# Weight units of the second block rounded and completed by GpSimd's own memory transfers

## The reference, cut to what matters

```python
h = rms_norm_2(x, norm_g)
proj = h @ w_in                                    # (512, 1024) @ (1024, 9 k)
(a_u, a_v, a_z, b_q, b_c, b_qi, b_ki, b_wi, b_z,
 c_b, c_c, c_x, c_z, d_q, d_k, d_v, d_f, d_z, gates) = jnp.split(proj, points, axis=-1)
y_a = chunked_spatial_gating(a_u, a_v, ...) * jax.nn.silu(a_z)
y_b = dsa_attention(b_q, b_c, b_qi, b_ki, b_wi, ...) * jax.nn.silu(b_z)   # top-k of scores, sparse attention
y_c = short_gated_conv(c_b, c_c, c_x, conv_w) * jax.nn.silu(c_z)
y_d = forgetting_attention(d_q, d_k, d_v, d_f, fox_b_f) * jax.nn.silu(d_z)
branch_d = jnp.einsum('nbsw,nwd->bsnd', ys, w_branch)
merged = jnp.sum(jax.nn.sigmoid(gates) * branch_d, axis=2)
return x + merged @ w_out
```

## Time and profile before

| | |
|---|---|
| time, median of 3 runs | 1111.63 us (1111.48 to 1111.64) |
| span of the profiled execution, first to last instruction | 1109.4 us |
| busy: TensorE / VectorE / ScalarE / GpSimd | 1100.7 / 744.2 / 506.9 / 19.8 us |
| weight loads of TensorE | 931.1 us |
| read from memory, written | 115.74 MB, 4.19 MB |
| mean rate, share of the 16 engines used by SyncE's queue | 109 GB/s, 29.7% |

### The profile page before, as it was taken

How to read it: one execution, slowest core, us unless ns; L and a number is a source line. 1 busy time by engine, 2 the same in 40 slices (tenths; PEclk the granted TensorE clock), 3 DMA queues, 4 the chain that set the end, 5 groups by cost and what they waited for, 6 DMA issues and landing times.

```text
span 1109.4 us, 18066 instructions
## 1 busy us (share of the span) xinstructions
PE 1100.7 (99%) x7344; PEld 931.1 (84%) x7344; DVE 744.2 (67%) x1195; ACT 506.9 (46%) x851; POOL 19.8 (2%) x40
## 2 busy tenths in 40 slices
PE   9999999999999999999999999999999999999997
PEld 8888888888888888878888887887789999999986
DVE  6875876864686247448789896447568677667853
ACT  7562354324675225533342434336544444444543
POOL 1000000000001001000000000000000000000000
PEclk9999999999999999999999999999999999999999
DMA  9543324432215433522223232231121322333241
GB/s 372 220 149 125 125 68 133 127 102 73 74 58 167 139 95 111 185 74 79 77 76 95 77 95 68 66 114 58 58 73 61 114 93 80 115 115 114 81 186 76
DMA packets 33618, 121.09 MB, mean 109 GB/s; under 512 B 3824, under 2 KB 3824, under 8 KB 33536
## 3 DMA queue, kind: packets, MB, share of 16 engines
q1 hardware_dynamic: 30672, 109.88, 29.7%
q0 software_dynamic: 2720, 10.03, 2.7%
q10 hardware_dynamic: 144, 0.03, 0.0%
HBM read 115.74 MB, written 4.19 MB: 108 GB/s over the span
## 4 chain that ended last, share of the span: by engine, by line
PE 98%; DMA 1%; DVE 1%; ACT 0%; SPq 0%; issue 0%; ACTq 0%
PE acc L1829 22%; PE acc L1831 21%; PE acc L1830 21%; PE acc L1841 2%; PE side L1841 2%; PE acc L1839 2%; PE side L1839 2%; PE acc L1837 2%; PE side L1837 2%; PE acc L2189 2%; PE side L1829 2%; PE side L1830 2%; PE side L1831 2%; PE side L2071 2%; PE side L1984 2%; PE side L2189 1%
## 5 line engine op out<-in xcount | busy, mean ns | idle before, releaser
L1160 DVE TENSOR_TENSOR w_lo<-raw,w_hi 128x1024 fp32r<-128x1024 f32 (+2 forms) x194 | 225.8, 1165 | 149.7 <-ACT w_hi L649 146.8
L1829 PE MATMUL acc<-hT_hi,w_hi 128*128 128x512 f32 x648 | 258.9, 400 | 0.0
L1831 PE MATMUL acc<-hT_hi,w_lo 128*128 128x512 f32 x648 | 252.8, 390 | 0.0
L1830 PE MATMUL acc<-hT_lo,w_hi 128*128 128x512 f32 x648 | 252.4, 390 | 0.0
L649 ACT ACTIVATE w_hi<-raw 128x1024 fp32r<-128x1024 f32 (+2 forms) x194 | 195.6, 1009 | 115.4 <-PE acc L1831 87.7
L1829 PEld LDWEIGHTS acc<-hT_hi,w_hi 128*128 128x128 f32 x648 | 121.9, 188 | 26.9 <-issue 2.9
L1831 PEld LDWEIGHTS acc<-hT_hi,w_lo 128*128 128x128 f32 x648 | 121.6, 188 | 26.1
L1830 PEld LDWEIGHTS acc<-hT_lo,w_hi 128*128 128x128 f32 x648 | 121.9, 188 | 23.6
L1829 PE MATMUL acc<-w_hi,hT_hi 128*128 128x512 f32 (+1 forms) x152 | 60.3, 396 | 0.0
L1831 PE MATMUL acc<-w_hi,hT_lo 128*128 128x512 f32 (+1 forms) x152 | 58.8, 387 | 0.0
L1830 PE MATMUL acc<-w_lo,hT_hi 128*128 128x512 f32 (+1 forms) x152 | 58.7, 386 | 0.0
(11 more groups left out here) (461 smaller groups left out, 2251.5 us busy)
## 6 DMA issues: line engine op xcount, KB each, us to landing
raw<-in_ga SPq DMA_DIRECT2D x32, 512.0 KB, 4.5
ada_raw<-in_ada SPq DMA_DIRECT2D x16, 512.0 KB, 11.5
raw<-in_wo SPq DMA_DIRECT2D x16, 512.0 KB, 3.5
raw<-in_br SPq DMA_DIRECT2D x16, 512.0 KB, 3.5
raw<-in_q SPq DMA_DIRECT2D x8, 512.0 KB, 3.5
raw<-in_u SPq DMA_DIRECT2D x8, 512.0 KB, 4.0
raw<-in_gp SPq DMA_DIRECT2D x8, 512.0 KB, 4.5
raw<-in_ada_w SPq DMA_DIRECT2D x8, 512.0 KB, 3.6
```

What stands on the lines that cost most here:

```text
L1160: nc.vector.tensor_tensor(out=lo[:, 0:width], in0=strip_of(k), in1=hi[:, 0:width].bitcast(f32), op=ALU.subtract).then_inc(lo_made, 1)
L1829: nc.tensor.matmul(ps, w[0], x[0], start=first, stop=False)
L1830: nc.tensor.matmul(ps, w[0], x[1], start=False, stop=False)
L1831: return nc.tensor.matmul(ps, w[1], x[0], start=False, stop=last)
```

## The change

The 44 units leave `ORDER`, so SyncE no longer loads them and they no longer pass through `raw`. GpSimd gets a loop over them (`FED`). For a unit k it waits until `unit_used` is k - 3 and issues a transfer from memory straight into `w_hi`, whose type makes the transfer round. ScalarE, where it rounded before, waits for that transfer and writes -w_hi into `w_lo`. GpSimd waits for that (`negated`), and for the last adding transfer before it (`fed_lo`), and issues a second transfer of the same unit into `w_lo` that adds: w_lo = w - w_hi. TensorE waits for this one. VectorE's subtraction is gone for these units. `parts_made(k)` counts the units up to k that are still made in the old way; waits on `hi_made` and `lo_made` use it.

```diff
+FED_KINDS = ("au", "az", "cc", "cx", "cb", "cz", "dq", "dk", "dv", "bz", "dz")
+UNITS = [u for u in ORDER if u[0] not in ADA]
+ORDER = [u for u in ORDER if u[0] not in FED_KINDS]
...
+FED = [k for k, u in enumerate(USED) if u[0] in FED_KINDS]
+def parts_made(k):
+    return sum(1 for n in range(k + 1) if n not in FED)
+def fed_before(k):
+    return FED.index(k) + 1
...
@@ SyncE
-                        sp.wait_ge(lo_made, raw_done(last) + 1)
+                        sp.wait_ge(lo_made, parts_made(raw_done(last)))
...
@@ GpSimd, behind the loop that cuts the score tiles
+            for k in FED:
+                kind, j = USED[k]
+                pool.wait_ge(unit_used, k - SPLITS + 1)
+                pool.dma_start(w_hi[:, k % SPLITS, :], dram[kind][j, :, :]).then_inc(fed_hi, 16)
+                pool.wait_ge(negated, fed_before(k))
+                if fed_before(k) > 1:
+                    pool.wait_ge(fed_lo, 16 * (fed_before(k) - 1))
+                pool.dma_start(w_lo[:, k % SPLITS, :], dram[kind][j, :, :], accum_op=ALU.add).then_inc(fed_lo, 16)
...
@@ ScalarE, split_hi
+                if k in FED:
+                    act.wait_ge(fed_hi, 16 * fed_before(k))
+                    nc.scalar.activation(w_lo[:, k % SPLITS, :], w_hi[:, k % SPLITS, :].bitcast(f32), ACT.Copy, scale=-1.0)\
+                        .then_inc(negated, 1)
+                    return
...
@@ VectorE, split_lo
+                if k in FED:
+                    return
-                dve.wait_ge(hi_made, k + 1)
+                dve.wait_ge(hi_made, parts_made(k))
...
@@ TensorE, weights
-                if first:
-                    pe.wait_ge(lo_made, k + 1)
+                if first and k in FED:
+                    pe.wait_ge(fed_lo, 16 * fed_before(k))
+                elif first:
+                    pe.wait_ge(lo_made, parts_made(k))
```

More of the change, by code:

```diff
@@ L55 @@
 USED = []
-for u in ORDER:
+for u in UNITS:
     if u[0] == "br" and u[1] >= FIRST_PAIR:
         USED += [("sa", u[1]), ("sb", u[1]), u, ("sc", u[1]), ("sd", u[1])]
-    elif u[0] not in ADA and not (u[0] == "ga" and u[1] >= 2 * FIRST_PAIR):
+    elif not (u[0] == "ga" and u[1] >= 2 * FIRST_PAIR):
         USED.append(u)
@@ L408, in program @@
         hi_made, lo_made = sem("hi_made"), sem("lo_made")
+        fed_hi, fed_lo, negated = sem("fed_hi"), sem("fed_lo"), sem("negated")
         ada_summed, strip_weighed, mod_ready = sem("ada_summed"), sem("strip_weighed"), sem("mod_ready")
@@ L1179, in combine @@
                     dve.wait_ge(combined, 3 * (n - 1) + 1)
-                    dve.wait_ge(lo_made, STEP["sa", j] + 1)
+                    dve.wait_ge(lo_made, parts_made(STEP["sa", j]))
                     nc.vector.tensor_tensor(out=a[:, 512:1024], in0=a[:, 512:1024], in1=s12[:, 1, :], op=ALU.subtract)\
@@ L2199, in lower_w @@
                         return head_part(h, lo, hT_hi, False, True)
-                    pe.wait_ge(hi_made, k + 1)
+                    pe.wait_ge(hi_made, parts_made(k))
                     pe.wait_ge(h_hi, j + 1)
```

## The result

The changed kernel takes 1192.0 us (median of three, 1191.3 to 1195.4) against 1111.6 before: a ratio of 1.073, 95% interval 1.071 to 1.075. The forecast was slower, 1179 us, in a range of 1120 to 1299. The profiled execution spans 1193.7 us, 84.3 more than before.

A forecast was written before the change was run, and what follows sets the result against it. TensorE was taken to bound the kernel; GpSimd's serial loop at 8.5 us per unit would replace its pace in the 44 steps, adding 67 us to 1111.6, so 1178.6, given as 1179 us, range 1120 to 1299.

The forecast's parts named there:

- The bound before: Stage of the 44 steps: TensorE sets the pace, 296.95 of 297.4 us busy; relieving VectorE gives back at most 0.5 us.
- The beat: GpSimd's loop over the 44 units: serial length P per unit, taken as 8.5 us between 8.25 and 8.9.
- three links: GpSimd's loop: rounding flight behind the adding transfer 6.9 to 7.54 us, ScalarE's copy 1.05, two hand-overs of 0.15 each.
- the second way of counting: Rounding transfer's flight in GpSimd's loop: 1.25 us data per 512 KB, adding bytes twice, fixed 3.15; sum 6.9 us.
- From the beat to the time: Stage of the 44 steps: at P = 8.5 the delay is 44 us at unit 105, 67 at unit 124; the larger counts.
- the formula: End of unit n on TensorE when the loop runs at P: 508.6 + (n - 81) P.
- The sum for unit 105: Delay at unit 105, ending at 668.3 before: 24 P - 159.7, 44 us at P = 8.5; break-even P = 6.65.
- ScalarE's new wait: Head of ScalarE's step, waiting for unit k + 3's transfer: other work, 1.8 us, fits the 6.9 us flight; nothing added.
- What would show it: Changed profile: adding transfers 8.5 us apart, TensorE waiting for w_lo, rounding landing 6.9 us, stage 364 us, VectorE 54 less.
- slow rounding or adding in the memory engines: Rival for the loop's transfers: P over 10; at 12.0 the time is +217 us, 1329; chance 20%.
- Nearly free transfers: Rival for the loop's transfers: P about 7.0, price +4 to +27 us; chance 17%.
- Hidden altogether: Rival for the loop: P under 6.65, rounding transfer landing by 4.4 us, price 0 to 2 us; chance 9%.

The follow-up runs named there:

- e4: The changed kernel with the second transfer of each unit rounding into w_lo instead of adding to it; 1130.8 us, ratio 1.017.
- e3: The changed kernel without the adding transfers, so the lower part stays -w_hi and TensorE waits for the negation; 1113.7 us, ratio 1.0018.
- e9: The changed kernel with bz and dz, the last 8 fed units, made the old way again, so the loop serves 36 units; 1173.3 us, ratio 1.055.
- e6: The changed kernel with both the early rounding transfer of e1 and the late negation of e2; 1110.7 us, ratio 0.9992 to the kernel before.
- e2: The changed kernel with ScalarE's negating copy moved from the head of the step to behind its own and attention work; 1184.7 us, ratio 1.065.
- e5: The changed kernel with only the 22 odd-numbered units going the new way, the other 22 the old way; 1122.3 us, ratio 1.010.
- e1: The changed kernel with unit k + 1's rounding transfer issued before GpSimd waits for the negation of unit k; 1114.3 us, ratio 1.0024.

## Why the prediction was right, point by point

**The bound before**: right. TensorE's own work filled the stage, and taking 51 us from VectorE gave nothing back.

**The beat**: forecast 8.5 us, measured 8.43. Its three links held. The flight of a rounding transfer behind an adding one, from the latter's issue, was put at 6.9 to 7.5 us and is 0.56 + 6.45 = 7.01 in the mean. The copy is 1.06 us, and the two hand-overs, for which no row was shown, are 0.03 and 0.33 us instead of 0.15 each. Inside the flight two errors offset each other. An adding transfer was counted with its bytes twice, 3.14 us, and took 3.04 (e4). A rounding transfer was bounded between the plain price and twice that, and costs little more than the plain one: 1.67 to 1.82 us of data, 3.8 us to land alone (e3), where I had used the 4.4 of the row of before. So the fixed part is 3.8 - 1.67 = 2.1 us and not 2.83 to 3.15, and the two data terms are 4.7 us, where the second way of counting, nearer to which I stayed, had 3.75. That 8.5 came so near was partly luck. An issue held GpSimd for 0.85 us with the add, and for as long when it stood directly behind one, instead of 0.56; it lies beside the flight and is not in the beat. The rule of the Trainium skill ("Collectives: The Full Stack", Part 3) that an add in a memory engine costs its second read, and not its arithmetic, agrees with e4 as far as the size goes, 3.04 against 1.67 us; no run tells the read from the arithmetic. The formula of the Trainium skill ("DMA: Bandwidth & Descriptors", Anatomy of one DMA) gives an estimate of 3.2 us for a 512 KB transfer of this queue; e3 says 3.8.

**From the beat to the time**: the formula, with 8.43, puts the end of unit 116 at 508.6 + 35 x 8.43 = 803.7, and it is 804.2. In between TensorE is up to 10 us later than the formula (unit 99 ends at 670.6, formula 660.3) and catches up again. By mean steps of 7.34 us I had let the loop stay the bound up to unit 124. Steps 119 to 122 took 8.6 to 10.1 us before, more than the beat, so the loop's worst point is unit 119 (828.9 against 761.6, 67 us late), and the delay then stays. At 8.43 this is worth 3.5 us on the 63.8 of unit 124. The forecast also cut the pace by the starts of result copies, some of which come 3 us and more after the unit's end: by TensorE's own products the steps 102 to 105 take 25.0 us, 6.3 each and not 5.45, and are not bare of attention work (the logits L2087 are in them at 661.20). The sum for unit 105 doesn't suffer, because its own copy starts at its end.

**ScalarE's new wait**: this is the step that failed: "So I add nothing in the forecast", with the reason that its other work fits into the flight. It does fit on average, 1.8 us beside 6.9. But it isn't spread: a chain of probabilities goes from TensorE to ScalarE, VectorE and back, in some steps more than once, and each time that it meets ScalarE in front of the negation it stands for up to 8 us. While the loop is the bound anyway this costs nothing that lasts (unit 116 is where the beat alone puts it). Where the work behind it is longer than the beat, at steps 117 and on, it is lost: some 17 us. e9 shows that this loss hangs on the loop being still at work at step 117; that it comes through ScalarE's queue is read from the timelines above and borne out by e4, where 9.9 us are lost at unit 117 with TensorE waiting for no `w_lo`, and by e6, where nothing is lost. Together: 67 us by the beat and the long steps, and some 17 us by ScalarE's wait, make the 84.6 of the trace. The profiled execution was the slowest of the three; by the medians the change is 80.4 us, forecast 67.

**What would show it**: the distances on GpSimd's timeline and the untouched stages came as said. The rounding transfer took 6.3 us from its own issue instead of 6.9, VectorE lost 51 us instead of 54, and the stage was 382 us long instead of 364. That TensorE would wait for transfers into `w_lo` did not: 3.1 us of it, because ScalarE is later than the weights. By the prediction's own test ("I am wrong if ... TensorE's new waits are for ScalarE") the way was wrong. That the cause behind it was the loop is shown by its beat, which ScalarE never delays, and by e2 and e5; e1 and e3 agree. e2 shows besides that the name of the releaser hangs on the order in ScalarE's queue.

**The rivals**: slow rounding or adding in the memory engines is excluded by e3 and e4, a limit of the engines' rate by e1 (0.71 of the stage busy, at nearly the time of before). Nearly free transfers are what e4 shows without the add, beat 6.6 us where the loop runs free: the price was forecast as 4 to 27 us and is 19, half of it from ScalarE's wait at unit 117. Hidden altogether is e3 and e6.

Left open is what the lower clock costs ahead of unit 117, and why e6 is 0.9 us below the kernel before, within its interval; 0.5 us of it arise at unit 105, in front of which the kernel before waits 0.3 us for `sel`.

## What to carry to other kernels

A queue that issues a transfer, waits for what depends on it and issues the next has a beat, and the beat is a sum over the whole ring of waits; compare it with the consumer's shortest and longest steps, not with its mean, and ask which wait can stand one turn later. Here one issue moved ahead of one wait was worth 78 of 80 us. When a wait is put at the head of an in-order engine's step, everything behind it inherits the delay, and the profile will name that engine and not the transfer: look up what ended the idle time of the engine that is named.

## What was not expected of the hardware

Rounding on the way costs a transfer of GpSimd's queue little: 1.67 us (by e4) to 1.82 us (by e3) of the engines' time for 512 KB, against 1.57 for its plain transfers before, and 3.8 us to land. Adding on the way costs 3.04 us, 5.5 us to land, and holds GpSimd for 0.85 instead of 0.55 us. After gaps of 14.2 and 5.5 us TensorE's units took 7.5 and 7.3 instead of 5.7 us, at a mean granted clock of 0.74 and 0.77, so part of each at the lower of its two levels (1.2 and 2.4 GHz).
